# Another order of the mixer stage: conv projections first, conv tiles in a row, pooling last, and the sample convolution by products and sums

## The reference, cut to what matters

```
u = hn @ w_in[l]                                   # 1536 columns: 512 pool, 512 value, 512 gate
pool_out = per group g: (window mean(2,4,8,16) of u_pool - u_pool) @ pool_w[g] * scale
v = value * sigmoid(gate); ext = concat(past 30 rows, v)
y = depthwise causal convolution of ext, 31 taps, + bias; y = silu(layernorm(y))
conv_out = y @ conv_pw_w
h = h + concat(pool_out, conv_out) @ w_out[l]
```

## Time and profile before

| | |
|---|---|
| median of 3 runs | 1609.77 us (1607.04 to 1610.88) |
| the profiled execution | 1608.4 us, its span 1606.6 us |
| busy share of the span | PE 95%, DVE 78%, ACT 61%, POOL 11% |
| mixer stage of layer 0 | 27.2 to 181.3 us |
| mixer stage of layer 1 | 428.6 to 588.9 us |
| dense SwiGLU, experts | between the two, and from 608.6 us on |

### The profile page before, as it was taken

The page is one execution under the profiler, slowest core; times in us unless marked ns, Lnnn a source line. Parts: engine busy times, 40 slices in busy tenths (PEclk is TensorE's granted clock), DMA queues, the critical chain, the costliest instruction groups (busy, mean ns, idle before and its releaser), DMA issues.

```text
span 1606.6 us, 21672 instructions
## 1 busy us (share of the span) xinstructions
PE 1520.1 (95%) x7823; PEld 1321.6 (82%) x7823; DVE 1259.8 (78%) x1295; ACT 980.2 (61%) x969; POOL 174.7 (11%) x224
## 2 busy tenths in 40 slices
PE   4968999999997889999999999999999999999995
PEld 4968999999996887888888888888888888888884
DVE  4797765544479758888888888888888888888887
ACT  3644343333454427777777777777777777777773
POOL 4033500001103317400000000000000000000002
PEclk8988999999998889999999999999999999999997
DMA  6124799435122429999999999999999999999993
GB/s 189 61 78 129 215 323 289 138 124 171 53 70 69 154 74 349 392 386 360 379 365 376 367 364 379 377 354 378 369 366 367 378 363 375 370 364 374 381 359 109
DMA packets 243521, 447.39 MB, mean 278 GB/s; under 512 B 8886, under 2 KB 93942, under 8 KB 243472
## 3 DMA queue, kind: packets, MB, share of 16 engines
q1 hardware_dynamic: 239280, 436.83, 76.3%
q0 software_dynamic: 2960, 9.73, 2.0%
q10 hardware_dynamic: 1231, 0.19, 0.1%
HBM read 421.60 MB, written 25.12 MB: 278 GB/s over the span
## 4 chain that ended last, share of the span: by engine, by line
issue 56%; PE 4%; POOL 3%; DVE 3%; DMA 2%; ACT 0%; DVEq 0%; POOLq 0%; ACTq 0%
PE ps L1505 1%; PE ps L1506 1%; PE ps L1507 1%; POOL h L738 1%; DVE y L1081 1%; POOL og L747 1%; DMA xg<-og,row_i 1%; POOL xg L714 0%; DMA last_row<-last_pos 0%; DMA og<-obuf,out_row_i 0%; DMA h<-last_row 0%; POOL key L726 0%; DVE w_lo L494 0%; PE ps L1680 0%; ACT hn L928 0%
## 5 line engine op out<-in xcount | busy, mean ns | idle before, releaser
L506 DVE TENSOR_TENSOR w_lo<-raw,w_hi 128x2048 fp32r<-128x2048 f32 x336 | 769.7, 2293 | 130.2 <-ACT w_hi L501 128.4
L501 ACT ACTIVATE w_hi<-raw 128x2048 fp32r<-128x2048 f32 x336 | 643.4, 1915 | 133.7 <-PE ps L1507 133.7
L1505 PE MATMUL ps<-w_hi,xg_hi 128*128 128x512 f32 x896 | 355.5, 397 | 4.5 <-DVE xg_lo L1426 4.5
L1507 PE MATMUL ps<-w_hi,xg_lo 128*128 128x512 f32 x896 | 354.1, 395 | 0.0
L1506 PE MATMUL ps<-w_lo,xg_hi 128*128 128x512 f32 x896 | 354.0, 395 | 0.0
L1505 PEld LDWEIGHTS ps<-w_hi,xg_hi 128*128 128x128 f32 x896 | 168.5, 188 | 47.3 <-issue 7.7
L1505 PE MATMUL ps<-x_hi,w_hi 128*128 128x336 f32 x580 | 191.0, 329 | 12.5 <-DVE x_lo L1241 7.1
L1507 PEld LDWEIGHTS ps<-w_hi,xg_lo 128*128 128x128 f32 x896 | 168.4, 188 | 40.4
L1506 PEld LDWEIGHTS ps<-w_lo,xg_hi 128*128 128x128 f32 x896 | 168.5, 188 | 39.7
L1506 PE MATMUL ps<-x_lo,w_hi 128*128 128x336 f32 x580 | 188.2, 325 | 0.0
L1507 PE MATMUL ps<-x_hi,w_lo 128*128 128x336 f32 x580 | 188.2, 325 | 0.0
(11 more groups left out here) (249 smaller groups left out, 1876.3 us busy)
## 6 DMA issues: line engine op xcount, KB each, us to landing
raw<-in_moe_w_gate_dram SPq DMA_DIRECT2D x112, 1024.0 KB, 7.3
raw<-in_moe_w_up_dram SPq DMA_DIRECT2D x112, 1024.0 KB, 7.6
raw<-in_moe_w_down_dram SPq DMA_DIRECT2D x112, 1024.0 KB, 7.4
raw<-in_w_in_dram SPq DMA_DIRECT2D x12, 1024.0 KB, 5.0
raw<-in_ffn_w_gate_dram SPq DMA_DIRECT2D x11, 1024.0 KB, 6.0
raw<-in_ffn_w_up_dram SPq DMA_DIRECT2D x11, 1024.0 KB, 6.4
raw<-in_w_out_dram SPq DMA_DIRECT2D x8, 1024.0 KB, 5.1
obuf<-ones SPq DMA_DIRECT2D x15, 512.0 KB, 7.8
```

The source lines that it names most:

```text
L501: nc.scalar.activation(hi, r, ACT.Copy).then_inc(hi_done, 1)
L506: nc.vector.tensor_tensor(lo, r, hi.bitcast(F32), ALU.subtract).then_inc(lo_done, 1)
L1505: nc.tensor.matmul(out, a_hi, b_hi, start=start, stop=False)
L1507: return nc.tensor.matmul(out, a_lo, b_hi, start=False, stop=stop)
```

## The change

It does these things in each layer.

- Slots: all four value and gate slots of `w_in` come first (0 to 3), then d0 to d5 (4 to 9), then the two pool slots (10, 11), pointwise (12), `pool_w` (13).
- PE: value 0, gate 0, past states, value 1, gate 1, conv tiles 0, 2, 3 in a row, mean, pool 2/3, variance, pool 0, spread, pool 1, pointwise, all four pool maps, `w_out` (which takes its inputs in the order pointwise, pool 2, 3, 0, 1).
- `ACT_DIAG = (0, 1, 4, 5)`: ACT writes the high diagonals of d4 and d5 too; DVE only those of d2 and d3.
- Samples: for each tile, twice (four sequences each), one `tensor_tensor` of all windows times all taps (4 x 8 x 31 = 992 products for each partition) and one `tensor_reduce` over the taps; then one `tensor_scalar` for the bias.
- Prompt columns of tile 1: one chain, each instruction waiting for the one before.
- DVE's `pooled_low` and `m_low` and ACT's `pooled_high` and `m_high` follow the new order of PE.
- `pool_in` of all four groups comes after the mean on DVE, and so all of POOL's window work.

```diff
-    W_AT, D_AT = (0, 1, 2, 5, 6, 11), (3, 4, 7, 8, 9, 10)
-    S_POOL_W, S_PW, S_OUT = 12, 13, 14
-    ACT_DIAG = 2
+    W_AT, D_AT = (0, 1, 2, 3, 10, 11), (4, 5, 6, 7, 8, 9)
+    S_PW, S_POOL_W, S_OUT = 12, 13, 14
+    ACT_DIAG = (0, 1, 4, 5)
...
-        M_ORDER = (*POOL_ORDER[:2], *range(NG, KD), *POOL_ORDER[2:])
+        M_ORDER = (*range(NG, KD), *POOL_ORDER)
...
@@ mixer_layer of ACT @@
-                split_to(b + W_AT[2])
-                split_to(b + D_AT[0])
+                split_to(b + W_AT[3])
                 gated(0)
-                split_to(b + D_AT[2])
+                split_to(b + D_AT[1])
                 gated(1)
-                split_to(b + D_AT[4])
-                pooled_high(POOL_ORDER[0])
-                split_to(b + D_AT[5])
-                pooled_high(POOL_ORDER[1])
                 split_to(b + S_PW)
...
+                pooled_high(POOL_ORDER[0])
+                split_to(b + S_POOL_W)
+                pooled_high(POOL_ORDER[1])
                 split_to(b + S_OUT)
-                pooled_high(POOL_ORDER[2])
                 for m in range(KC):
-                    if m == KC - 1:
-                        pooled_high(POOL_ORDER[3])
+                    if m == 2:
+                        pooled_high(POOL_ORDER[2])
                     m_high(("pw", l, m), NG + m, 1.0)
-                for g in POOL_ORDER[2:]:
+                pooled_high(POOL_ORDER[3])
+                for g in POOL_ORDER:
                     m_high(("pool", l, g), g, col(l, PSC, g))
...
@@ mixer_layer of DVE @@
+                def conv_prompt(c, taps):
+                    src, dst = conv_ext[:, c], y[:, c, 0:TP]
+                    for j in taps:
...
+                            link(nc.vector.scalar_tensor_tensor(dst, src[:, j:j + TP], tap(l, c, j), dst,
+                                                                ALU.mult, ALU.add))
+                def conv_samples(c):
...
+                    for i in (0, 1):
+                        past = samples(conv_ext[:, c, CSEG:CEXT])[:, HB * i:HB * (i + 1), :]
+                        windows = bass.AP(past.tensor, past.offset, [*past.ap[0:2], [1, DS], [1, TAPS]])
+                        link(nc.vector.tensor_tensor(prod_s, windows, taps, ALU.mult))
+                        out = y[:, c, TP + HB * DS * i:TP + HB * DS * (i + 1)]
+                        link(nc.vector.tensor_reduce(out.rearrange("p (b t) -> p b t", b=HB), prod_s, AX.X, ALU.add))
+                    link(nc.vector.tensor_scalar(y[:, c, TP:T], y[:, c, TP:T], col(l, DWB, c), None, ALU.add))
...
-                split_to(b + D_AT[1])
-                conv(OWN, range(0, 6))
+                split_to(b + W_AT[3])
+                conv_samples(DVE_TILE)
+                conv_samples(PE_TILES[0])
                 value(1)
-                split_to(b + W_AT[3])
-                conv(OWN, range(6, 12))
-                split_to(b + W_AT[4])
-                conv(OWN, range(12, 17))
+                gate(1)
+                gated(1)
+                split_to(b + D_AT[2])
+                conv_prompt(DVE_TILE, range(0, 8))
+                split_to(b + D_AT[3])
+                conv_prompt(DVE_TILE, range(8, 14))
                 conv_from_pe(PE_TILES[0])
-                split_to(b + D_AT[2])
-                gate(1)
-                split_to(b + D_AT[3])
-                gated(1)
-                for i in (0, 1):
-                    pool_in(4, i)
-                conv(OWN, range(17, 22))
-                split_to(b + D_AT[4])
-                conv(OWN, range(22, TAPS))
+                conv_prompt(DVE_TILE, range(14, TAPS))
                 dve.sem_inc(y_ready, 2)
                 split_to(b + D_AT[5])
-                conv(OTHERS, range(PE_TAPS[-1]))
-                conv(OTHERS + [(PE_TILES[-1], True)], range(PE_TAPS[-1], TAPS))
+                conv_samples(PE_TILES[1])
+                split_to(b + W_AT[4])
+                conv_samples(PE_TILES[2])
+                conv_prompt(PE_TILES[2], range(PE_TAPS[-1], TAPS))
                 conv_from_pe(PE_TILES[1])
                 split_to(b + W_AT[5])
                 conv_from_pe(PE_TILES[2])
-                split_to(b + S_POOL_W)
...
-                for g in POOL_ORDER[:2]:
-                    pooled_low(g)
+                pool_in(4, 0)
+                split_to(b + S_PW)
+                pool_in(4, 1)
                 rstd_by_token(("var", l), CW, 1e-5)
                 pool_in(5, 0)
-                split_to(b + S_PW)
...
@@ mixer_layer of PE @@
                 w_in_slot(2)
+                w_in_slot(3)
                 for q, c in enumerate(PE_TILES):
-                    if q == 1:
-                        w_in_slot(3)
-                        w_in_slot(4)
...
+                w_in_slot(4)
+                token_sums(("var", l), z[:, 0, :], sq_sum, l + 1)
                 w_in_slot(5, (0,))
-                token_sums(("var", l), z[:, 0, :], sq_sum, l + 1)
+                spread(("spread var", l), 2 * l + 2)
                 w_in_slot(5, (1,))
-                spread(("spread var", l), 2 * l + 2)
-                split_ready(b + S_POOL_W)
-                for g in POOL_ORDER[:2]:
-                    pool_map(g)
                 split_ready(b + S_PW)
...
-                for g in POOL_ORDER[2:]:
+                split_ready(b + S_POOL_W)
+                for g in POOL_ORDER:
                     pool_map(g)
```

More of the change, by code:

```diff
@@ L107, in hybrid_trunk @@
         plan(("past_pool", l), ("past_conv", l, 0), ("past_conv", l, 1))
[L108 to L112, removed]
+        plan(*[("win", l, 2 * s + i) for s in WIN_ORDER[2:4] for i in (0, 1)])
+        plan(*[("conv", l, c) for c in PE_TILES])
+        plan(*[("win", l, g) for g in POOL_ORDER], *[("pw", l, m) for m in range(KC)])
+        plan(*[("pool", l, g) for g in POOL_ORDER])
         for m in range(KD):
@@ L284, in hybrid_trunk @@
         packed = sem("packed")
-        rw_landed, conv_step = sem("rw_landed"), sem("conv_step")
+        rw_landed = sem("rw_landed")
         gate_scaled, silu_done = sem("gate_scaled"), sem("silu_done")
@@ L355, in dense_slots @@
                 out += [mix[at] for at in range(12)]
+                out.append(blk(conv_pw_w[l], 0, KC, 0, CW))
                 out.append((pool_w[l].rearrange("g p n -> p g n"), NG, P))
-                out.append(blk(conv_pw_w[l], 0, KC, 0, CW))
                 out += [blk(w_out[l], 0, KD, 256 * s, 256) for s in range(4)]
@@ L483, in split_lo_dense @@
                 l, k = DIAG[n]
-                if k >= ACT_DIAG:
+                if k not in ACT_DIAG:
                     (_, _, c, a), taps, _ = SLOTS[n]
@@ L1065, in mixer_layer @@
                 b = MIX_BASE[l]
-                def conv(chains, taps):
+                def conv_prompt(c, taps):
+                    src, dst = conv_ext[:, c], y[:, c, 0:TP]
                     for j in taps:
[L1070 to L1083, removed]
@@ L1085, in mixer_layer @@
-                OWN = [(DVE_TILE, True), (DVE_TILE, False), (PE_TILES[0], False)]
-                OTHERS = [(PE_TILES[1], False), (PE_TILES[2], False)]
+                        if j == (PE_TAPS[-1] if c == PE_TILES[-1] else 0):
+                            link(nc.vector.tensor_scalar(dst, src[:, j:j + TP], tap(l, c, j), col(l, DWB, c),
+                                                         ALU.mult, ALU.add))
+                        else:
+                            link(nc.vector.scalar_tensor_tensor(dst, src[:, j:j + TP], tap(l, c, j), dst,
+                                                                ALU.mult, ALU.add))
@@ new lines, in conv_samples @@
+                def conv_samples(c):
+                    at = 64 + (l * KC + c) * TAPS
+                    taps = params[:, at:at + TAPS].unsqueeze(1).unsqueeze(1).broadcast_to([P, HB, DS, TAPS])
+                    prod_s = z[:].rearrange("p k t -> p (k t)")[:, 0:HB * DS * TAPS].rearrange(
+                        "p (b t j) -> p b t j", b=HB, t=DS)
+                    for i in (0, 1):
[5 more added lines that the diff above has]
+                    link(nc.vector.tensor_scalar(y[:, c, TP:T], y[:, c, TP:T], col(l, DWB, c), None, ALU.add))
@@ L1243, in mixer_layer @@
                 dve.sem_inc(sums_read, 1)
-                for g in POOL_ORDER[:2]:
-                    m_low(("pool", l, g), g, col(l, PSC, g))
+                pooled_low(POOL_ORDER[0])
+                split_to(b + S_POOL_W)
+                pooled_low(POOL_ORDER[1])
                 split_to(b + S_OUT)
-                pooled_low(POOL_ORDER[2])
                 for m in range(KC):
-                    if m == KC - 1:
-                        pooled_low(POOL_ORDER[3])
+                    if m == 2:
+                        pooled_low(POOL_ORDER[2])
                     m_low(("pw", l, m), NG + m)
-                for g in POOL_ORDER[2:]:
+                pooled_low(POOL_ORDER[3])
+                for g in POOL_ORDER:
                     m_low(("pool", l, g), g, col(l, PSC, g))
@@ L1279, in mixer_layer @@
```

(6 more changed lines are left out.)

10 lines of the change are left out of this document (3 added, 7 removed).

## The result

The changed kernel takes 1597.15 us (median of 4 executions, 1596.66 to 1597.55) beside 1608.4 of the kernel before on the same chip (1605.29 to 1610.88). The ratio is 0.9931, with an interval of 0.9911 to 0.995: faster by 0.7%. The forecast was 1604.3 in a range of 1597 to 1615, so the time lies at the very edge of the range. The spans of the two profiled executions are 1595.3 and 1606.6: the gain to be explained is 11.3 us, where the forecast had 5.5. From such a base the gain would be some 9 us, so times that were taken on different chips compare only to within about 2 us.)

A forecast was written before the change was run, and what follows sets the result against it. PE's entry into w_out was taken to bound the mixer's gain: 4.4 us in layer 0 plus 4.1 in layer 1, 8.5, less 2 x 1.5 for the clock, 5.5. Against the 1609.8 median: 1604.3 us, range 1597 to 1615.

The forecast's parts named there:

- What bounds the kernel: Experts and dense SwiGLU run at PE's own pace; a mixer edit is worth what it moves PE's entry into w_out.
- The conv stage: Convolution up to the mean: ACT's diagonals set the pace; last mean sum at 112.1 us instead of 123.4.
- The slack ahead of the tanh: In the convolution, DVE waits for ACT's tanh until 69.4, with 5.4 us of slack.
- The price of a product and of a reduce: DVE's samples: each 992-element product or reduce costs 1.22 us, with 0.66 as lower and 2.3 as upper bound.
- the slack ahead of slot 10: Late in the convolution, DVE waits from 97.3 to 100.4 for slot 10: 3 us of slack.
- The contention: Beside POOL's window means DVE's 15 taps lose 4.8 us, a diagonal slot more; the change removes this from the convolution.
- the clock price at w_out: After PE's wait at w_out, a lower clock costs 1.5 us a layer, range 0 to 3.1.
- The POOL chain: Behind the mean, POOL's window work runs from 120.0 to 145.3: 20.8 us plus 4.5 for three splits.
- 147.1, set by POOL: w_out can start at 147.1 us, after POOL's chain and hand-overs, with PE waiting between 1 and 3 us.
- The third rival: No price at w_out: PE hardly idles, clock stays up; gain 8.5 to 12.5 us, 1597.3 to 1601.3; chance 0.25.
- The first rival: In the tail, short DVE instructions also hold POOL, 4.7 us; w_out at 151.8, time 1613.7 us; chance 0.12.
- The factors' chain: DVE's small factor instructions behind the mean take 3.0 us, up to 2 more with POOL active.

The follow-up runs named there:

- the slot moved up: Changed kernel with the slots of d0 and gate 1 changed round, so ACT can write d0 sooner; 1593.18 us, ratio 0.9912.
- the diagonals moved back: Changed kernel with the high diagonals of d4 and d5 written by DVE again, behind the tap chain; 1604.8 us in one execution.
- chains: Changed kernel, its order kept, with the samples of each pair of tiles made by linked tap chains again; 1601.11 us, ratio 0.9966.
- the samples beside it: Old-order kernel with product-and-reduce samples; last two sample tiles moved beside POOL's first windows, 14 prompt taps behind them; 1589.61 us, ratio 0.9885.

## Why the prediction was right or wrong, point by point

**What bounds the kernel: right.** All of the gain is in PE's entry into w_out: 11.6 us, of which the span shows 11.3, and nothing was won in the experts.

**The conv stage: right within 1.7 us.** The last mean sum was forecast at 112.1 and came at 110.39. That ACT sets the pace up to the tanh is shown by DVE's wait there and by the slot moved up (4.0 us); that DVE has next to no room behind it, by the diagonals moved back (7.6 us). The 1.7 us are mostly ACT's: a diagonal comes every 0.29 us and not every 0.30 (31 from 70.30 to 79.37), and DVE could start slot 10 at 98.95 where the forecast had 100.4. The slack ahead of the tanh was 5.62 for 5.4. The samples made twice in the first place disappear in it. The price of a product and of a reduce was 1.22 and measured 1.19. The tap of 272 columns is 0.54 and not 0.47: 30 of them ahead of slot 10 cost DVE 30 x 0.065 = 2 us more, which went into the slack ahead of slot 10 (0.98 left of 3). The Trainium skill, "VectorE: DVE Perf Modes", section "Rules for kernel authors", calls the reduce the engine's slowest operation; here, over 992 elements of 4 bytes, it takes as long as the product.

**The contention: right.** It was put at 4.8 us of taps and more for a diagonal slot. With POOL's sums gone the last mean sum is 6.1 sooner: 4.3 for the 15 taps, 1.0 for the diagonal slot, 0.8 for the taps behind it. The entry is 6.6 and 6.8 sooner.

**The step that failed is the clock price at w_out**, put at 1.5 us a layer (0 to 3.1). It measured nothing: the clock is 1.00 from 145.50, and PE's wait there is 0.2 us. The two were one mistake. I had PE wait 1 to 3 us for POOL's chain, and from that wait the price of the clock. The POOL chain itself was well forecast in length (25.3 for 25.0) but began 1.8 us sooner, because the mean was sooner, and ended at 143.2. And PE's own work was as late as it: pointwise ended at 143.92, within the forecast of 142.5 to 144.6. With POOL's windows left out, PE still waits 0.2 at that place. The step "147.1, set by POOL" should have read: 146 in layer 0 and 144.7 in layer 1, set by PE's own chain. It was close: in other executions of this tail (one slot earlier, diagonals back, last samples twice, chains) PE waits 0.3 to 0.8 us there in layer 0, so POOL's chain is off the path by less than 1 us. The entries came 6.1 us sooner than forecast: 3.0 for the clock price, 0.9 and 2.2 for the entry of each layer. The third rival was the case that took place. It gave a gain of 8.5 to 12.5 us, and the measured 11.3 is in the upper part of that, for the 1.7 us by which the conv stage ended sooner. The measured gain is twice the forecast one; that the time lies in the range is owed to this rival, at whose end the range was drawn. That the median lies just below its 1597.3 comes from the base: the kernel before ran at 1608.4 beside it, 1.4 under the 1609.8 that I took off from.

**The first rival**, that short instructions of DVE hold POOL up too, showed itself only in small pieces: beside the products of three numbers POOL's two sums took 1.0 us each, and beside the pointwise low parts of 336 columns one sum took 1.24 for 0.97 and a piece of 0.2 took 0.45. The whole of POOL's chain was not longer than forecast. It is DVE's small instructions that pay. The factors' chain was forecast at 3.0, up to 2 more, and took 5.2; of three equal products one took 0.81 and one 0.17. The 0.81 ended at 123.28, when POOL's second sum had ended at 123.25: such a DVE instruction, started beside one of POOL's, waits that one out. PE waited 1.7 for the factors, which the forecast had as a possibility and not in the sum. Products of 1.2 us do hold POOL, as the samples beside it show.

**What the prediction did not ask is what each part is worth without the other.** It priced the new order as one thing with the samples. The stretches of PE show what the order does when the samples are the same. First the kernel with slices and sums in the old order, then the changed one, from value 1 to the last mean sum and from there to w_out:

```profile
47.68:118.07 70.39, 62.75 (x429) 0.93 0.24 79
118.07:144.60 26.53, 22.48 (x119) 0.87 0.47 153
```

```profile
46.46:110.39 63.93, 52.76 (x381) 0.99 0.32 104
110.39:146.06 35.67, 31.41 (x167) 0.88 0.36 115
```

48 matmuls, the projection of pool 2/3, go from the first stretch to the second. The first loses 10.0 us of busy PE, but its idle time grows from 7.6 to 11.2, since that work had filled gaps of the diagonals: it is 6.5 shorter. The second has 8.9 us more of busy PE and idle time as before (4.1 and 4.3): it is 9.1 longer. Net 2.7 us lost in layer 0, and in layer 1 98.19 for 97.31. So the order, which gains 8.7 us of entry with chains, costs 2.7 + 0.9 = 3.6 with slices. The spans differ by 2.9 (1595.3 for 1592.4) in the same direction; the intervals of the two ratios overlap, so it is the stretches that show it, each from one execution. The reason that fits is that the order's merit was to take taps away from POOL, and with slices there are few left to take. That last step is argued from the counts, not shown by a run of its own.

**Two equal layers, two clocks.** The stretch behind the mean takes 10.71 us in layer 0 and 9.77 in layer 1 with equal work, at mean clocks of 0.75 and 0.83. The stretch from the last sum but one to the last mean sum, in which PE mostly waits (length, busy, granted clock), shows where the difference comes from:

```profile
107.50:110.39 2.89, 0.84 (x3) 0.76 0.00 0
502.16:505.04 2.88, 1.49 (x2) 0.50 0.00 0
```

In layer 1 the clock stands at the lower level (0.50) for all of this stretch, in layer 0 for about half of it. So in layer 1 more of the lower level falls on time in which PE is idle anyhow, and less is left for the matmuls behind.

**Left open.** What makes the clock fall 2 us earlier in one layer than in the other. And no run here tried the new order with a tail of another sequence.

## What to carry to other kernels

Price the parts of a change separately and in each other's absence: here one part alone was as good as both, and the second gained 8.7 us of entry (5.2 of time) without the first and cost 3.6 of entry with it. A piece of PE work is cheapest where PE has gaps; moved behind a point at which all engines meet, it is paid in full and perhaps at the lower clock. Beside POOL put reduces or work with an input in PSUM, and ahead of a known wait put whatever is long.

## What the runs showed of the hardware that was not expected

A reduce over [32, 31] of 4-byte elements takes 1.19 us, exactly as long as the product of 992 columns, and the product from overlapping windows lies where the line through other shapes put it (1.19 for 1.22). A linked tap of 272 columns comes every 0.54 us, one of 336 every 0.54 too, so the line through 336 and 2048 columns doesn't hold below 336 for a linked pair.

Beside POOL's work a DVE instruction of two inputs in SBUF grows and a reduce does not: taps of 64 and 272 columns together from 4.61 to 8.92 us for 15, a product of 992 from 1.19 to between 1.57 and 1.95, while a reduce stays at 1.19. One input alone is no protection: the `tensor_scalar` of 64 columns took 0.39 and 0.48 there for 0.26. The Trainium skill, "SBUF — State Buffer", section "Who interferes with whom", has the pair of SBUF ports that the two engines share as an exclusive lock. The trace agrees, in both directions. Beside a split of 2.28, POOL's sum at 118.22 took 2.94 for its usual 0.97. And the short DVE instructions that grew ended just after the POOL instruction beside them had: 0.81 for 0.17 at 123.28 for POOL's 123.25, and 0.72 for 0.17 at 125.08 for 125.06. Who loses more is a matter of length: DVE's short ones wait out POOL's of 1.0 us, and POOL loses little to them (1.08 and 1.16 a sum beside taps, 1.42 and 1.64 beside products and reduces). An input in PSUM did not count: the four y<-y,ps of 336 columns took 1.75 us beside POOL's sums (127.98), as they do elsewhere.
